# A two-block transformer kernel on one core: weight parts at a pitch of 1028 words, x_high's tiles at 514

## The chip, the cores and the metric

The kernel runs on one core of a Trainium2 chip. The metric is the device time of one execution in microseconds; the time before is 3353.7 us, the median of 3 runs from 3351.68 to 3357.03. Engines go by the names of the profile: PE is TensorE (its weight loads, LDWEIGHTS, are listed apart as PEld), ACT is ScalarE, DVE is VectorE, POOL is GpSimd, SP is SyncE, which issues the DMAs.

## What is computed

Two blocks follow each other, with two layers each, on one sequence of 512 rows with 1024 columns. Cut to what matters here, a layer of the first block is

```python
h = x @ w_in[l]                      # 1024 -> 10016 columns
# four branches of 512 columns: a recurrence, latent attention, a convolution, attention into 256 memory rows
proj = jnp.einsum('bsnc,ncd->bsnd', branches, w_o_branch[l])
merged = jnp.sum(gates * proj, axis=2)      # gates: sigmoid of 4096 columns of h
x = _layer_norm(DEEPNORM_ALPHA * x + merged @ w_out[l], ln_g[l], ln_b[l])
```

and a layer of the second block (which also carries a context of 256 rows, in its first layer through everything, in its second as keys and values only)

```python
zx = hx @ w_in[i]                    # hx: x normed and modulated
mx = concat([latent_attention(...), pool_mix(...), fourier_mix(...)])
x = x + ga1 * (mx @ w_out[i])
x = x + ga2 * swiglu(fx, w_gate_up[i], w_down[i])   # 1024 -> 2 x 2816 -> 1024
```

All of it is float32. The large products are done in three matmuls each: both operands are split into a high part, which the PE takes in its fp32r form, and a low part, the rest; and high x high, high x low and low x high are added up in PSUM.

## The kernel before, in words

**Weights.** All weights of the large products come as chunks of 128 x 1024 words (512 KB), one DMA each, into `ring`, which has three slots. For a chunk that is split, ACT copies the slot to a slot of `highs` (line 123) and POOL subtracts and writes a slot of `lows` (line 131). `highs` and `lows` have two slots each (`PARTS = 2`); split chunks take them in turn, so that every other chunk of a product lies in slot 1. 376 chunks are split.

**Products.** Activations lie transposed, with the 1024 columns of x on 8 tiles of 128 partitions x 512 words: `x_high[:, k, :]` and `x_low[:, k, :]`, k from 0 to 7. For one chunk, the usual order on the PE is 16 matmuls that take `highs` as the stationary operand, with x_high and x_low as the moving one in turn (lines 155 and 158, in `with_high`), and then 8 that take `lows` against x_high (line 723 in the first block, 2140 in the second). The stationary tile of step k is 128 words wide and lies k * 512 bytes into the slot (`tile_of`). Where operands come late, and for `w_out` and `w_down`, all three matmuls of a step k stand together (lines 163, 166 and 167, in `three`). The same two orders run over other activations: `branches_high/low` and `merged_high/low` in the first block (512 columns wide), `context_high/low` (256 wide), `mixed_parts` and `hidden_parts` (512 wide for x, 256 for the context) in the second.

**What sets the order.** Every engine's instructions are written out by hand with semaphores. `Stream.send` issues the DMA of a chunk when its slot of `ring` is free, `Stream.hi` makes the high part on ACT once the chunk of two places earlier has been used, and `Stream.lo` follows on POOL. The PE waits for a high part at the start of a chunk (`wait_high`) and for the low part after the first 16 matmuls (`wait_split`).

**The other matmuls** (the recurrence, both attentions, transposes, small products) take plain float32 operands, such as `ring` itself as the moving operand in line 1544.

**Where tensors lie.** Every tensor has a start address in each partition, and they are laid down one behind another. All moving and stationary operands of the split products start at a multiple of 64 bytes before the change: tiles have a pitch of 2048 bytes (1024 for the context), slots of 4096, and stationary tiles of 512.

Of the kernel before, what the change touches and what calls it, by code (L numbers as in the profile page):

```python
# [17 lines left out]
F32R = mybir.dt.float32r  # L18
# [4 lines left out]
P = 128  # L23
T = 512
D = 1024
DK = D // P
# [14 lines left out]
RING = 3  # L41
PARTS = 2
CW = 1024
# [131 lines left out]
def build(nc, A):  # L175
    with ExitStack() as ctx:
        def sb(name, shape, dt=F32):
            return ctx.enter_context(nc.sbuf_tensor(name, shape, dt))

        pools = [[nc.alloc_semaphore(f"stage{p}_{i}") for i in range(47)] for p in range(3)]  # L180
        arrived = [nc.alloc_semaphore(f"chunk_arrived{i}") for i in range(RING)]
        used = nc.alloc_semaphore("chunks_used")
        hi_made, lo_made = nc.alloc_semaphore("high_made"), nc.alloc_semaphore("low_made")
        loaded = nc.alloc_semaphore("loaded")
        stored = nc.alloc_semaphore("stored")
        constants = nc.alloc_semaphore("second_constants")
        PS = ctx.enter_context(nc.psum_tensor("ps", [P, 8, 512], F32))
        turn = [0]

        def stage():  # L190

            turn[0] += 1
            return Names(pools[turn[0] % 3]), pools[(turn[0] + 1) % 3]

        WR = (sb("ring", [P, RING, CW]), sb("highs", [P, PARTS, CW], F32R), sb("lows", [P, PARTS, CW], F32R),
              arrived, used, hi_made, lo_made)
        mods = sb("mods", [P, LAYERS, 96])

        XH, XL = sb("x_high", [P, DK, T], F32R)[:, :, :], sb("x_low", [P, DK, T], F32R)[:, :, :]
        BR = sb("BR", [P, NB * WT, T])  # L200

        def weights(n):
            if n < SECOND:
                return A["w1"][n // NCHUNK1, n % NCHUNK1, :, :]
            return A["w2"][n - SECOND, :, :]

        split = [NCHUNK1 * layer + n for layer in range(LAYERS) for n in SPLIT1] + SPLIT2
        stream = Stream(WR, weights, split)
        with ExitStack() as one:
            merged = first(nc, one, A, PS, XH, XL, BR, stream, mods, stage, loaded)  # L210
        with ExitStack() as two:
            second(nc, two, A, PS, XH, XL, BR, stream, mods, stage, constants, stored, merged)
# [2888 lines left out]
```

## Time and profile before

| what | value |
|---|---|
| median of 3 runs | 3353.7 us (3351.68 to 3357.03) |
| the profiled execution's own time | 3352.91 us |
| its span, first to last instruction | 3351.1 us |
| mean granted clock of the PE | 0.989 of full speed |
| PE busy | 3206.5 us, 96% |
| PE weight loads busy | 2516.6 us, 75% |
| DVE, ACT, POOL busy | 1508.9, 1183.9, 1485.4 us |

Busy time of the PE counts each matmul to its end, and a matmul of 512 columns is recorded with about 390 ns although the next one starts some 230 ns after it. So what one matmul costs in a dense stretch is read from start to start, over many of them, and not from its duration. A row of the timeline that holds several of one kind gives the start of the first and the time to the end of the last.

### The profile page before, as it was taken

How to read it: one execution, taken by the hardware profiler on the slowest of the kernel's cores; microseconds unless marked ns; L12 is line 12 of the kernel's file. 1: busy time of each engine (PE TensorE's matmuls, PEld its weight loads, DVE VectorE, ACT ScalarE, POOL GpSimd, SP SyncE). 2: the span in 40 equal slices, each digit the busy share in tenths (PEclk: the TensorE clock that was granted, in tenths of full speed). 3: DMA queues.
4: the chain of work that ended last, by engine and by line, in shares of the span. 5: the costliest groups of instructions: out<-in, count | busy, mean ns of one | idle time of the engine just before them, and what ended most of it. 6: DMA issues, size and time to landing. Idle time of an engine off the chain costs nothing. (4 is left out here: it accounts for less than half of the span.)

```text
span 3351.1 us, 51795 instructions
## 1 busy us (share of the span) xinstructions
PE 3206.5 (96%) x21120; PEld 2516.6 (75%) x21120; DVE 1508.9 (45%) x2374; ACT 1183.9 (35%) x1940; POOL 1485.4 (44%) x820
## 2 busy tenths in 40 slices
PE   8899999999999999999998989999999998999999
PEld 6784786888668747868876756788888875678787
DVE  7633374999575333949996235300100022520000
ACT  6224433422353434252225445322122243532221
POOL 4421553444353235545442276344234434745454
PEclk9999999999999999999999999999999999999999
DMA  3011132555220111235543200121122211023232
GB/s 130 8 34 57 57 101 76 208 201 191 78 63 4 46 63 64 94 114 196 206 151 109 66 26 27 51 64 63 57 70 63 63 61 51 16 80 101 92 97 94
DMA packets 77611, 284.18 MB, mean 85 GB/s; under 512 B 8736, under 2 KB 8736, under 8 KB 76864
## 3 DMA queue, kind: packets, MB, share of 16 engines
q1 hardware_dynamic: 77376, 280.88, 25.2%
q8 instruction: 168, 2.75, 0.3%
q14 instruction: 67, 0.55, 0.1%
HBM read 278.75 MB, written 2.10 MB: 84 GB/s over the span
## 5 line engine op out<-in xcount | busy, mean ns | idle before, releaser
L131 POOL TENSOR_TENSOR lows<-ring,highs 128x1024 fp32r<-128x1024 f32 x376 | 941.4, 2505 | 1542.5 <-ACT highs L123 1508.3
L155 PE MATMUL ps<-x_high,highs 128*128 128x512 f32 x2080 | 831.5, 400 | 33.7 <-ACT highs L123 14.9
L158 PE MATMUL ps<-x_low,highs 128*128 128x512 f32 x2080 | 814.3, 391 | 0.0
L123 ACT ACTIVATE highs<-ring 128x1024 fp32r<-128x1024 f32 x376 | 397.0, 1056 | 714.6 <-PE ps L155 375.8
L155 PEld LDWEIGHTS ps<-x_high,highs 128*128 128x128 f32 x2080 | 392.4, 189 | 133.6 <-issue 37.8
L158 PEld LDWEIGHTS ps<-x_low,highs 128*128 128x128 f32 x2080 | 392.8, 189 | 83.8 <-issue 4.8
L1790 DVE CUSTOM_DVE_ANT_0 BR<-BR 128x1024 f32<-128x1024 f32 x144 | 289.4, 2010 | 6.8
L2830 DVE TENSOR_TENSOR hidden_scratch<-ps,hidden_scratch 128x512 f32<-128x512 f32 x44 | 30.4, 691 | 546.5 <-PE ps L2140 538.3
L723 PE MATMUL ps<-x_high,lows 128*128 128x512 f32 x1024 | 252.9, 389 | 0.0
L723 PEld LDWEIGHTS ps<-x_high,lows 128*128 128x128 f32 x1024 | 192.2, 188 | 39.9
L2706 DVE SCALAR_TENSOR_TENSOR BR<-ps,mod,BR 128x512 f32<-128x512 f32 x72 | 47.3, 662 | 364.9 <-PE ps L167 364.9
L163 PE MATMUL ps<-hidden_parts,highs 128*128 128x512 f32 (+1 forms) x528 | 188.0, 356 | 0.0
L167 PE MATMUL ps<-hidden_parts,lows 128*128 128x512 f32 (+1 forms) x528 | 188.0, 356 | 0.0
L166 PE MATMUL ps<-hidden_parts,highs 128*128 128x512 f32 (+1 forms) x528 | 188.0, 356 | 0.0
L471 POOL TENSOR_SCALAR tiles<-tiles 128x768 f32<-128x768 f32 (+1 forms) x80 | 154.8, 1947 | 29.0 <-DVE tiles L498 29.0
L2140 PE MATMUL ps<-x_high,lows 128*128 128x512 f32 x672 | 167.1, 391 | 0.0
L1605 DVE SCALAR_TENSOR_TENSOR ps<-X,par,ps 128x512 f32<-128x512 f32 x232 | 152.9, 741 | 0.0
L2140 PEld LDWEIGHTS ps<-x_high,lows 128*128 128x128 f32 x672 | 123.3, 188 | 24.0
L471 POOL TENSOR_SCALAR X<-X 128x256 f32<-128x256 f32 (+3 forms) x96 | 97.7, 1030 | 67.3 <-DVE X L498 67.2
L492 DVE TENSOR_REDUCE tiles<-ps 128x1 f32<-128x768 f32 (+1 forms) x80 | 67.6, 845 | 109.2 <-PE ps L365 109.0
L166 PEld LDWEIGHTS ps<-hidden_parts,highs 128*128 128x128 f32 x528 | 99.4, 188 | 15.8
L163 PEld LDWEIGHTS ps<-hidden_parts,highs 128*128 128x128 f32 x528 | 99.2, 188 | 16.0
(443 smaller groups left out, 5584.6 us busy)
## 6 DMA issues: line engine op xcount, KB each, us to landing
ring<-in_w SPq DMA_DIRECT2D x414, 512.0 KB, 3.5
BR<-in_ada SPq DMA_DIRECT2D x72, 512.0 KB, 3.5
merging<-in_ada SPq DMA_DIRECT2D x24, 512.0 KB, 3.4
X<-in_xT SPq DMA_DIRECT2D x4, 512.0 KB, 6.5
X<-in_memT SPq DMA_DIRECT2D x2, 1024.0 KB, 5.3
BR<-in_cond SPq DMA_DIRECT2D x4, 512.0 KB, 4.7
out<-BR SPq DMA_DIRECT2D x8, 256.0 KB, 4.5
cst<-in_cst SPq DMA_DIRECT2D x1, 1408.0 KB, 8.0
```

The source lines that it names most:

```text
L123: nc.scalar.activation(self.high(n), self.chunk(n), ACT.Copy).then_inc(self.hi_made, 1)
L131: nc.gpsimd.tensor_tensor(self.low(n), self.chunk(n), self.high(n).bitcast(F32), ALU.subtract).then_inc(self.lo_made, 1)
L155: mm = nc.tensor.matmul(ps, high, xhigh, start=start, stop=False)
L158: nc.tensor.matmul(ps, high, xlow, start=False, stop=False)
L163: mm = nc.tensor.matmul(ps, high, xhigh, start=start, stop=False)
L166: nc.tensor.matmul(ps, high, xlow, start=False, stop=False)
L167: return nc.tensor.matmul(ps, low, xhigh, start=False, stop=stop)
L471: nc.gpsimd.tensor_scalar(prob(i, u), prob(i, u), stats[:, 3, n:n + 1], None, ALU.mult).then_inc(S("normed"), 1)
L723: mm = nc.tensor.matmul(PS[:, bank, :], tile_of(stream.low(n), k), xh[:, k, :], start=False, stop=(k == DK - 1))
L1605: ins = v.scalar_tensor_tensor(out=ACC[:, c, :] if tap == TAPS - 1 else acc, in0=H0[:, c, tap:tap + T], scalar=w, in1=acc, op0=ALU.mult, o ...
L1790: v.tensor_tensor_reduce(PROD, rows_of(t), CB[:, c, :], 1.0, 0.0, ALU.mult, ALU.add, AD[:, t, c:c + 1]).then_inc(S("ada"), 1)
L2140: mm = nc.tensor.matmul(ps, tile_of(stream.low(n), k), high[:, k, :], start=False, stop=(k == DK - 1))
```

## The change

The slots of `highs` and `lows` get a pitch of 1028 words in place of 1024, and the tiles of `x_high` one of 514 words in place of 512. The words that are added are never read or written: the views that the rest of the kernel uses are cut to the old widths.

```diff
-        WR = (sb("ring", [P, RING, CW]), sb("highs", [P, PARTS, CW], F32R), sb("lows", [P, PARTS, CW], F32R),
-              arrived, used, hi_made, lo_made)
+        ring, highs = sb("ring", [P, RING, CW]), sb("highs", [P, PARTS, CW + 4], F32R)
+        lows = sb("lows", [P, PARTS, CW + 4], F32R)
+        WR = (ring, highs[:, :, 0:CW], lows[:, :, 0:CW], arrived, used, hi_made, lo_made)
         mods = sb("mods", [P, LAYERS, 96])
 
-        XH, XL = sb("x_high", [P, DK, T], F32R)[:, :, :], sb("x_low", [P, DK, T], F32R)[:, :, :]
+        XH, XL = sb("x_high", [P, DK, T + 2], F32R)[:, :, 0:T], sb("x_low", [P, DK, T], F32R)[:, :, :]
```

No instruction is added, removed or moved: each engine has the same list in the same order (PE 9604 rows of the program, DVE 1808, ACT 1258, POOL 431, SP 322), each line number behind the change being higher by one. What changes are addresses. The start addresses, in bytes of a partition, with the remainder by 256 in brackets:

| tensor | before | after |
|---|---|---|
| highs, slot 0 / slot 1 | 28800 (128) / 32896 (128) | 28800 (128) / 32912 (144) |
| lows, slot 0 / slot 1 | 36992 (128) / 41088 (128) | 37024 (160) / 41136 (176) |
| x_high, tile k | 45952 + 2048k (128) | 46016 + 2056k (192 + 8k) |
| x_low | 62336 (128) | 62464 (0) |
| branches_high / branches_low | 158464 (0) / 125696 (0) | 158592 (128) / 125824 (128) |
| merged_high / merged_low | 212928 (192) / 196544 (192) | the same |
| context_high / context_low | 127744 (0) / 135936 (0) | 127872 (128) / 136064 (128) |
| mixed_parts, hidden_parts | 163648 (64), 147264 (64) | 163776 (192), 147392 (192) |

So the padding also moves what lies behind it: x_low and most later tensors lie 128 bytes further on. By 64 bytes, slot 1 of `highs` has the remainder 16, the slots of `lows` 32 and 48, and x_high's tile k has 8k; every other operand of the split products still has 0. Among the plain float32 matmuls, line 784 takes as its stationary operand a part of `par` that starts 56 bytes behind a multiple of 64, before as after.

## Rows read from the trace of the kernel before

**Rows 1.** The page: its head and first part, busy time of each engine.
```profile
span 3351.1 us, 51795 instructions
...
PE 3206.5 (96%) x21120; PEld 2516.6 (75%) x21120; DVE 1508.9 (45%) x2374; ACT 1183.9 (35%) x1940; POOL 1485.4 (44%) x820
```

**Rows 2.** The last chain, in order of time: start us, us, what.
```profile
3170.22 1.81 PE ps L2140 x8
3175.66 1.81 PE ps L2140 x8
3181.10 1.81 PE ps L2140 x8
```

**Rows 3.** PE timeline, start us, duration, line: x, then branches, then x.
```profile
1490.92 0.39 PE L155 MATMUL ps<-x_high,highs 128*128 128x512 f32 x1
...
1494.54 1.98 PE L723 MATMUL ps<-x_high,lows 128*128 128x512 f32 x8
1496.36 0.40 PE L155 MATMUL ps<-branches_high,highs 128*128 128x512 f32 x1
...
1501.95 0.39 PE L155 MATMUL ps<-x_high,highs 128*128 128x512 f32 x1
```

**Rows 4.** PE timeline: hidden_parts, 512 wide, and earlier 256 wide.
```profile
3158.04 0.40 PE L163 MATMUL ps<-hidden_parts,highs 128*128 128x512 f32 x1
...
3164.81 0.39 PE L167 MATMUL ps<-hidden_parts,lows 128*128 128x512 f32 x1
...
2663.10 0.28 PE L163 MATMUL ps<-hidden_parts,highs 128*128 128x256 f32 x1
...
2664.12 0.39 PE L163 MATMUL ps<-hidden_parts,highs 128*128 128x512 f32 x1
```

**Rows 5.** PE timeline: merged (two rows), then context, 256 wide.
```profile
888.20 0.39 PE L155 MATMUL ps<-merged_high,highs 128*128 128x512 f32 x1
...
891.86 1.99 PE L1844 MATMUL ps<-merged_high,lows 128*128 128x512 f32 x8
...
2214.31 1.12 PE L2140 MATMUL ps<-context_high,lows 128*128 128x256 f32 x8
2215.26 0.40 PE L155 MATMUL ps<-x_high,highs 128*128 128x512 f32 x1
```

**Rows 6.** Windows: us, busy of PE, PEld, DVE, ACT, POOL, granted clock, DMA.
```profile
1490.92:1496.36 5.44, 5.44 (x26) 4.51 (x25) 5.02 (x7) 5.40 (x9) 2.16 (x1) 1.00 0.65 220
...
3158.04:3164.81 6.77, 6.77 (x31) 5.46 (x29) 0.25 (x1) 1.06 (x1) 2.40 (x1) 1.00 0.00 0
1496.36:1501.95 5.59, 5.59 (x26) 4.51 (x24) 5.59 (x7) 4.05 (x7) 2.29 (x2) 1.00 0.79 288
```

**Rows 7.** PE timeline: a run of plain float32 matmuls (ring moving).
```profile
548.52 5.74 PE L1544 MATMUL ps<-ring,X 128*128 128x512 f32 x13
```

**Rows 8.** Two lines of plain float32 matmuls: durations ns, min/median/max.
```profile
L1544 PE MATMUL ps<-ring,X x64: 592/592/593, 542.9 to 1454.0; 128*128 128x512 f32 x64
...
L784 PE MATMUL ps<-X,par x16: 589/589/694, 27.5 to 932.4; 64*128 64x512 f32 x16
```

**Rows 9.** Groups on the PE, shapes apart: busy us, mean ns, idle before.
```profile
L155 PE MATMUL ps<-x_high,highs 128*128 128x512 f32 x2080 | 831.5, 400 | 33.7 <-ACT highs L123 14.9 <-ACT X L268 7.6 <-DVE x_low L611 5.1
L158 PE MATMUL ps<-x_low,highs 128*128 128x512 f32 x2080 | 814.3, 391 | 0.0
L723 PE MATMUL ps<-x_high,lows 128*128 128x512 f32 x1024 | 252.9, 389 | 0.0
L2140 PE MATMUL ps<-x_high,lows 128*128 128x512 f32 x672 | 167.1, 391 | 0.0
...
L167 PE MATMUL ps<-hidden_parts,lows 128*128 128x512 f32 x352 | 139.2, 396 | 0.0
...
L158 PE MATMUL ps<-context_low,highs 128*128 128x256 f32 x416 | 101.9, 283 | 0.0
...
L1717 PE MATMUL ps<-branches_high,lows 128*128 128x512 f32 x256 | 65.0, 395 | 0.0
L163 PE MATMUL ps<-mixed_parts,highs 128*128 128x512 f32 x128 | 52.1, 407 | 4.6 <-DVE mixed_parts L2702 4.6
```

**Rows 10.** Timelines of PE, ACT and POOL beside the chain's chunks.
```profile
3171.87 0.39 PE L155 MATMUL ps<-x_high,highs 128*128 128x512 f32 x1
...
3172.57 1.05 ACT L123 ACTIVATE highs<-ring 128x1024 fp32r<-128x1024 f32 x1
...
3173.70 2.39 POOL L131 TENSOR_TENSOR lows<-ring,highs 128x1024 fp32r<-128x1024 f32 x1 [3.01 <-ACT highs L123]
```

## The prediction, made before the changed kernel had run

> **What bounds the kernel now.** The page first [rows 1]: the PE is busy 96% of 3351.1 us, and no other engine half of it. So the end is set by how fast the PE gets through its matmuls wherever it doesn't wait. The last chain shows such a place [rows 2]: the 8 matmuls with `lows` come back at 3170.22, 3175.66 and 3181.10, every 5.44 us, and the chain runs from PE to PE. A chunk is 24 matmuls, so one costs 5.44/24 = 226.7 ns. The timeline of another stretch has the same [rows 3]: from 1490.92 to 1496.36, 24 matmuls over x.
>
> The reader should then see that this price isn't the same for all operands. In the next chunk of that timeline, with the same instructions over the branches, 24 matmuls take 1501.95 - 1496.36 = 5.59 us, 232.9 ns each. Over hidden_parts, 29 matmuls from 3158.04 to 3164.81 take 233.4 ns each [rows 4]. The granted clock is 1.00 in all three stretches [rows 6], which is the level of 2.4 GHz, and over hidden_parts the DMA share is 0.00, so neither clock nor transfers make the difference. At 2.4 GHz 512 columns last 213.3 ns: an fp32r matmul pays 13 to 20 ns on top. A plain float32 matmul doesn't: 13 rows of line 1544 take 5.74 us, less the 0.592 that the last one lasts [rows 7, 8], is 429 ns for each of 12, which is two passes of 214.5 ns.
>
> Two things differ between those stretches: tensor and address. By the table of addresses, moving minus stationary operand, taken by 256 bytes, is 0 for x (226.7 ns), 64 for merged, 128 for branches (232.9) and 192 for hidden_parts (233.4). Merged has 16 matmuls from 888.20 to 891.86, 228.8 ns [rows 5]. For 256 columns, 192 (hidden_parts) has 9 from 2663.10 to 2664.12, 113.3 ns [rows 4], and 128 (context) has 8 from 2214.31 to 2215.26, 118.8 ns [rows 5]. I read this as two streams in the SBUF, the moving operand and the stationary tile of the next matmul that is loaded meanwhile, which hold each other up by an amount that hangs on how their addresses lie to each other. It isn't proven: four distances, each with its own tensor.
>
> **The change, part by part.** No instruction goes, comes or moves. Three things can change the time.
>
> *First, new distances for the PE.* I price each by a straight line between the four measured ones (0: 226.7, 64: 228.8, 128: 232.9, 192: 233.4, 256 again 226.7). Counts are those of [rows 9] or follow from the code's order (lines 155, 158 and a third one have 416, 416 and 416 for the context; 163, 166 and 167 the same count each).
> - x_high against `highs` (2080 matmuls, [rows 9]): 64 + 8k in slot 0 and 48 + 8k in slot 1, on average 84: 230.1 ns, +3.4 each, +7.1 us.
> - x_low against `highs` (2080): it isn't padded, but moves by 128 bytes, to 128 and 112: 232.4 ns, +5.7 each, +11.9 us.
> - x_high against `lows` (1024 + 672 + 384 of other lines, 2080): 32 + 8k and 16 + 8k, on average 52: 228.4 ns, +1.7 each, +3.5 us.
> - branches (512 with `highs`, 256 with `lows`): from 128 to 0 and 240 with `highs`, 227.5 ns, and to 224 and 208 with `lows`, 230.9: -2.8 and -0.5 us.
> - hidden_parts and mixed_parts, 512 wide (3 x 352 and 3 x 128): from 192 to 64, 48, 32 and 16: 228.2 ns, -5.2 each, -7.5 us.
> - merged stays at 64 or comes to 48 to 16: -0.3 us.
> - 256 wide: context (1248) goes from 128 to about 0, hidden and mixed (720) from 192 to about 64. No row shows either distance at this width. The two that are shown lie 5.5 ns apart; I take half of that, down for context and up for the others: -3.4 and +2.0 us.
> Together +10.0 us. I count every matmul as lying in a dense stretch. The PE's idle time before line 155 is only 33.7 us over 2080 matmuls [rows 9], so this overstates little.
>
> *Second, starts off a 64-byte boundary.* 7 of 8 x_high tiles and three of four slots of weight parts now start there. A stream of 2048 bytes then touches 33 blocks of 64 bytes and not 32. Bounds: below, nothing, since line 784, whose stationary operand starts 56 bytes behind such a boundary, lasts 589 ns against 592 [rows 8]. Above, one block's worth of columns, 16 at 2.4 GHz or 6.7 ns, for 7/8 of the 4160 matmuls that move x_high: 24 us. That size is no accident of mine alone: 226.7 ns is 544 columns' time, 32 more than the matmul has, and 233.4 is 560, 48 more, so the chip seems to pay in steps of 16. I take a quarter, 6 us: the nearest row shows nothing, but its two slow passes are also those that pay nothing at any address.
>
> *Third, those who write and read the padded tensors.* ACT makes a high part in 1.05 us and POOL a low part in 2.39 [rows 10]. The chunk that starts at 3171.87 is followed by the next one at 3171.87 + 5.44 = 3177.31. The high part is done at 3173.62: 3.7 us to spare. The low part is done at 3176.09 and wanted 16 matmuls into that chunk, at 3180.94: 4.9 us. (The two rows are the parts made while that chunk runs.) Were POOL to take half as long again, 1.2 us more, it would still be hidden. I cost this at nothing; with the cover gone, 1 us for each of 376 chunks would show.
>
> **Sum.** 10.0 + 6 = +16 us. The profiled execution took 3352.9 us, span 3351.1; the median is 3353.7, 0.8 higher. I forecast 3370 us, 0.5% slower, with 3357 to 3395 as this case's own range: 10 alone or less if the lines between the distances are wrong by half, and all 24 of the second term and more above.
>
> **What the Trainium skill says against this.** The Trainium skill, "SBUF — State Buffer", Who interferes with whom, gives the PE two read ports, one for the moving operand and one for weight loads, independent, and says that PE and ACT never wait on anyone. The Trainium skill, "TensorE: Matmul & The Clock Gate", Back-to-back issue gap, gives N/2.4 + 2.5 ns, 215.8 for 512 columns. By these addresses would not matter, and the sum would be 0. The trace agrees for plain float32, 214.5 ns a pass, and not for fp32r, 226.7 to 233.4.
>
> **The rivals.**
> *Faster: the streams no longer meet.* If what costs 13 to 20 ns is that both streams ask for the same place by 64 bytes in the same moment, then different remainders end it. For it: all split operands have remainder 0 now, and all pay. Against it: a matmul moves 2048 bytes of each partition while 512 bytes of weights are loaded, so the two streams pass each other at every offset anyway, and distances that differ by whole multiples of 64 already change the price. One step less on all 6240 matmuls over x, 6.7 ns, is -42 us; with the gains above for branches, hidden and mixed, -11, it gives about 3301. The whole price gone, 11.9 ns for 6240, 18 for 2208 and some 10 for 2350 others, is -138 us, 3216. It decides as soon as x_low and x_high fall below 226.7 ns. Chance 0.31.
> *No change* (where the two pages' rules lead as well). The mechanism would be that the distances are not the cause and the tensors' place in the program is; then x stays at 226.7. Or losses on x and gains on the others cancel: -11 for branches, hidden and mixed against +22 for x lies within the error of my lines. 3347 to 3360. Chance 0.19.
> *Much slower: every start off the boundary costs a full step.* Then 24 us for x_high, and the weight slots make the stationary stream longer too, up to one step more for three quarters of 11,070 matmuls, 55 us. With the 10 of the distances about 3400 to 3440. Chance 0.10.
> The forecast has 0.40.
>
> **How the numbers follow.** About 0.2%, 7 us, can be told from no change. Of the forecast's 0.40, 0.36 is slower and 0.04 the same; of the second rival's 0.19, 0.15 is the same and 0.02 each faster and slower. With the others: slower 0.36 + 0.02 + 0.10 = 0.48, same 0.19, faster 0.31 + 0.02 = 0.33. The range reaches down to the one-step gain, 3305, which leaves out a third of the first rival, and up to 3405, which leaves out most of the third: 0.1 below, 0.08 above.
>
> **What the profile after would show.** The x chunk's period in the last chain tells most: above 5.44 us the forecast holds, at 5.44 the second rival, below it the first. Step by step: x_low's matmuls dearer than x_high's before; the branches chunk down from 5.59 towards 5.5 us; hidden_parts down from 233.4 towards 228 ns; the price of x_high's tiles with k (if the second term is real, k = 0 is cheaper than the rest); line 131 at 2.4 us and line 123 at 1.05. The prediction is wrong if the distance by 256 bytes isn't what sets the price, or if the price follows the remainder by 64.

## The result, and the profile after

The changed kernel takes 3373.26 us (median of 3 runs, 3371.72 to 3379.16), against 3353.7 before: a ratio of 1.0061, 95% interval 1.0038 to 1.0084. It is slower, by some 20 us, and 3 us slower than forecast.

The page's head and part 1 of the kernel after, which answer to [rows 1]. The same number of instructions run. The PE is busy 24 us longer (3230.3 against 3206.5), the DVE 12 us less, the others within 4 us of before.

```profile
span 3371.4 us, 51795 instructions
PE 3230.3 (96%) x21120; PEld 2520.1 (75%) x21120; DVE 1496.9 (44%) x2374; ACT 1184.1 (35%) x1940; POOL 1487.4 (44%) x820
```

The chain that ended last, kernel after, answering to [rows 2] (start us, us, what; line 2141 is line 2140 of before). Two chunks lie between the first row and the second, 11.14 us, and the short rows between are steps of the same chain. A chunk takes 5.57 us, 232.1 ns per matmul, where it took 5.44 and 226.7.

```profile
3193.79 1.88 PE ps L2141 x8
...
3204.93 1.88 PE ps L2141 x8
...
3216.08 1.88 PE ps L2141 x8
...
3227.23 1.88 PE ps L2141 x8
```

Windows of the kernel after (columns as in [rows 6]): a chunk over x, one over the branches, and two of the last chain. The granted clock is 1.00, the level of 2.4 GHz, in all of them, as it was before. In the last one the vector engines and transfers do little (DMA share 0.29), and a chunk over x is as dear as where they are busy (0.69). So neither of them made it dearer.

```profile
1503.24:1508.80 5.56, 5.56 (x25) 4.52 (x24) 5.14 (x7) 5.52 (x9) 2.38 (x1) 1.00 0.69 206
1508.80:1514.40 5.60, 5.60 (x25) 4.54 (x24) 5.45 (x9) 3.92 (x7) 2.01 (x2) 1.00 0.84 296
3193.79:3204.93 11.14, 11.14 (x49) 9.02 (x49) 0.69 (x1) 3.13 (x4) 4.79 (x3) 1.00 0.29 95
```

PE timeline of the kernel after, over hidden_parts, to be held against [rows 4]. From 3164.74 to 3182.78 stand 78 matmuls, 231.3 ns each. It was 233.4 and was to become 228.2.

```profile
3164.74 0.39 PE L167 MATMUL ps<-hidden_parts,lows 128*128 128x512 f32 x1
...
3182.78 0.39 PE L167 MATMUL ps<-hidden_parts,lows 128*128 128x512 f32 x1
```

The costliest groups of the kernel after, answering to [rows 9, 10]. The PE's rows of x grew in mean duration by 2 to 7 ns. ACT's and POOL's writers of weight parts stand at 1057 and 2510 ns for all 376 chunks, where the page of before has 1056 and 2505 ns; their work stays beside the PE's.

```profile
L131 POOL TENSOR_TENSOR lows<-ring,highs 128x1024 fp32r<-128x1024 f32 x376 | 943.4, 2510 | 1559.5 <-ACT highs L123 1523.6
L155 PE MATMUL ps<-x_high,highs 128*128 128x512 f32 x2080 | 836.4, 402 | 29.1 <-ACT highs L123 10.5
L158 PE MATMUL ps<-x_low,highs 128*128 128x512 f32 x2080 | 824.1, 396 | 0.0
L123 ACT ACTIVATE highs<-ring 128x1024 fp32r<-128x1024 f32 x376 | 397.1, 1057 | 734.2 <-PE ps L155 396.4
...
L724 PE MATMUL ps<-x_high,lows 128*128 128x512 f32 x1024 | 260.5, 396 | 0.0
...
L2141 PE MATMUL ps<-x_high,lows 128*128 128x512 f32 x672 | 170.8, 396 | 0.0
```

**Where the 20 us are.** The PE runs its 21,120 matmuls in the same order in both traces, so the time from each start to the next can be compared one by one. Of the span's +20.3 us, +28.6 lie in dense stretches over x: x_high with `lows` +13.0, x_low with `highs` +10.3, x_high with `highs` +5.3. In five places of before, 1.0 to 1.7 us pass from the start of the last matmul of the branches with `lows` to the next one over x, with the PE idle; after the change 0.23 us does, and that gave 5.2 back. All else together is -3.

**The price by class.** The table has the mean time from start to start in ns, over all matmuls of a class in dense stretches (its own gap and the eight before it under 250 ns), worked out from each trace; the numbers of the experiments are told below. Under it stands the distance (moving minus stationary start, by 256 bytes). A gap is put down to the matmul that starts it. Where two classes alternate, as x_high and x_low do with `highs`, that is a convention: their mean is sure, which of the two is the dear one isn't.

| class | before | after | shift_only | behind128 | behind64 | behind32 | weights_only | x_tiles_only |
|---|---|---|---|---|---|---|---|---|
| x_high, highs | 227.7 | 230.4 | 234.3 | 233.9 | 229.2 | 233.6 | 231.0 | 231.8 |
| distance | 0 | 48 to 120 | 64 | 128 | 64 | 32 | 64, 48 | 0 to 56 |
| x_low, highs | 227.3 | 232.6 | 230.0 | 231.3 | 229.0 | 233.1 | 230.7 | 231.7 |
| distance | 0 | 128, 112 | 128 | 128 | 64 | 32 | 64, 48 | 0 |
| x_high, lows | 227.5 | 233.9 | 231.0 | 232.8 | 229.4 | 233.2 | 230.8 | 230.3 |
| distance | 0 | 16 to 88 | 64 | 128 | 64 | 32 | 32, 16 | 0 to 56 |
| hidden, highs, 512 wide | 233.1 | 231.9 | 228.8 | 228.1 | 228.1 | 233.3 | 234.4 | 228.0 |
| distance | 192 | 64, 48 | 64 | 64 | 0 | 224 | 0, 240 | 0 |

### The profile page after: what moved, and what is told of

Same layout as the page of the kernel before. It is cut to its first block and busy times, and to the rows that moved or that the text cites. A ratio compares the mean times of both kernels' runs of the same rounds, so it can differ in the third digit from the quotient of the medians.

```text
span 3371.4 us, 51795 instructions
## 1 busy us (share of the span) xinstructions
PE 3230.3 (96%) x21120; PEld 2520.1 (75%) x21120; DVE 1496.9 (44%) x2374; ACT 1184.1 (35%) x1940; POOL 1487.4 (44%) x820
## 5 line engine op out<-in xcount | busy, mean ns | idle before, releaser
L131 POOL TENSOR_TENSOR lows<-ring,highs 128x1024 fp32r<-128x1024 f32 x376 | 943.4, 2510 | 1559.5 <-ACT highs L123 1523.6
L155 PE MATMUL ps<-x_high,highs 128*128 128x512 f32 x2080 | 836.4, 402 | 29.1 <-ACT highs L123 10.5
L158 PE MATMUL ps<-x_low,highs 128*128 128x512 f32 x2080 | 824.1, 396 | 0.0
L123 ACT ACTIVATE highs<-ring 128x1024 fp32r<-128x1024 f32 x376 | 397.1, 1057 | 734.2 <-PE ps L155 396.4
L1791 DVE CUSTOM_DVE_ANT_0 BR<-BR 128x1024 f32<-128x1024 f32 x144 | 278.7, 1935 | 6.8
L724 PE MATMUL ps<-x_high,lows 128*128 128x512 f32 x1024 | 260.5, 396 | 0.0
L2141 PE MATMUL ps<-x_high,lows 128*128 128x512 f32 x672 | 170.8, 396 | 0.0
L167 PEld LDWEIGHTS ps<-hidden_parts,lows 128*128 128x128 f32 x528 | 99.1, 188 | 15.8
L163 PEld LDWEIGHTS ps<-hidden_parts,highs 128*128 128x128 f32 x528 | 99.2, 188 | 15.6
```

The source lines that it names most:

```text
L123: nc.scalar.activation(self.high(n), self.chunk(n), ACT.Copy).then_inc(self.hi_made, 1)
L131: nc.gpsimd.tensor_tensor(self.low(n), self.chunk(n), self.high(n).bitcast(F32), ALU.subtract).then_inc(self.lo_made, 1)
L155: mm = nc.tensor.matmul(ps, high, xhigh, start=start, stop=False)
L158: nc.tensor.matmul(ps, high, xlow, start=False, stop=False)
L163: mm = nc.tensor.matmul(ps, high, xhigh, start=start, stop=False)
L167: return nc.tensor.matmul(ps, low, xhigh, start=False, stop=stop)
```

## The experiments

### Whole multiples of 64 bytes only

Four kernels. The first shifts tensors as the change does but keeps every start on a 64-byte boundary. The second puts all tensors behind `lows` 128 bytes further. The third puts the weights and all behind them 128 bytes further, so that no distance changes except those to merged_high and merged_low, which lie at fixed places. The fourth takes from the change only the pitch of the weights' slots.

```diff
 shift_only
+        sb("pad", [P, 16])
         mods = sb("mods", [P, LAYERS, 96])
...
+        sb("pad2", [P, 16])          # between x_high and x_low
 behind128
+        sb("pad", [P, 32])
         mods = sb("mods", [P, LAYERS, 96])
 before_ring128
+        sb("pad", [P, 32])
         WR = (sb("ring", [P, RING, CW]), sb("highs", [P, PARTS, CW], F32R), sb("lows", [P, PARTS, CW], F32R),
 weights_only
+        ring, highs = sb("ring", [P, RING, CW]), sb("highs", [P, PARTS, CW + 4], F32R)
+        lows = sb("lows", [P, PARTS, CW + 4], F32R)
+        WR = (ring, highs[:, :, 0:CW], lows[:, :, 0:CW], arrived, used, hi_made, lo_made)
```

> No pitch changes; 64 bytes of padding behind lows and 64 behind x_high, so that every tensor starts at the same remainder by 256 as in the change (x_high 192, x_low 0, branches and context 128, hidden_parts 192) while all operands stay on 64-byte boundaries. Theory A (the distance of moving and stationary operand by 256 bytes sets the price): x_high 228.8 ns a matmul, x_low 232.9, branches 226.7, hidden_parts 228.8; about +10 us, 3364. Theory C (only the remainder by 64 matters): nothing changes, 226.7 for x, 3354. Rival B (the price belongs to the tensor's place in the program, not its address): 3354 as well, and branches stay at 232.9.

> 128 bytes of padding between lows and all that follows, all on 64-byte boundaries: both x tensors at distance 128, branches and context at 0, hidden_parts at 64, merged unchanged at 64. Theory A: x 232.9 ns (+39 us over 6240 matmuls), branches 226.7 (-5 us), hidden_parts and mixed_parts 228.8 (-7 us): about 3381. Theories B and C: 3354, x at 226.7.

> 128 bytes of padding ahead of ring: the weight slots and everything behind them move together, so the distances of x, branches, context and hidden_parts stay and only merged's (which is laid down from the other end) goes from 64 to 192. If the distance sets the price (A): x at 226.7 ns, merged at 233.4, 3355 in all. If it is the moving operand's own address by 256: the same as the kernel with 128 bytes behind lows, x at 232.9 and 3381.

> Only highs and lows get the pitch of 1028 words. Distances: x against highs 64 and 48, against lows 32 and 16; branches and context 192 and 176 against highs, hidden_parts 0 and 240. Theory A alone: x 228.5 with highs and 227.5 with lows (+9 us), hidden and mixed -7, context -6 or so: about 3350. If a weight slot's start off a 64-byte boundary costs by itself, the matmuls with lows stand at 232 ns or above instead of 227.5 and those of highs' slot 1 above those of slot 0: 3365 or more.

Measured: shift_only 3364.87 us, ratio 1.0035 (1.0022 to 1.0048). behind128 3368.06, 1.0040 (1.0026 to 1.0053). before_ring128 3353.45, 1.0004 (0.9994 to 1.0013). weights_only 3364.92, 1.0039 (1.0024 to 1.0054).

Only before_ring128 came out as expected in every part. shift_only met its 3364, but by luck: x_high with `highs`, at distance 64, cost 234.3 ns and not 228.8, x_low at 128 cost 230.0 and not 232.9. behind128 missed its 3381 by 13 us: its x matmuls, all at 128, cost 231.3 to 233.9, so that the dense stretches over x grew by 30 us where 39 were expected, and 4 us of waits behind the branches went. weights_only came out at the 3365 of the theory that a start off a boundary costs, but not by its price: with `lows` x cost 230.8 where that theory had 232 or more and the distance by straight lines 227.5.

The last chain of behind128, one chunk a row: 5.57 or 5.58 us, as after the change, with no start off a 64-byte boundary.

```profile
3233.83 1.86 PE ps L2141 x8
3239.41 1.86 PE ps L2141 x8
3244.98 1.86 PE ps L2141 x8
3250.56 1.87 PE ps L2141 x8
```

PE timeline of before_ring128 over merged_high and merged_low, to be held against [rows 5]. The distance went from 64 to 192. From 873.08 to 876.81 stand 16 matmuls, 233.1 ns each, where it was 228.8.

```profile
873.08 0.40 PE L155 MATMUL ps<-merged_high,highs 128*128 128x512 f32 x1
...
876.81 0.40 PE L1845 MATMUL ps<-merged_high,lows 128*128 128x512 f32 x1
```

What follows: in before_ring128 nearly everything moved and x, branches and hidden kept their prices (227.4, 237.1, 233.1); only the class whose distance changed changed its price. So the place and the tensor's part in the program don't set the price; how moving and stationary operand lie to each other does. It isn't the matmul's own distance alone, though: x_high at 64 costs 234.3 in shift_only and 229.2 in behind64, where x_low is at 64 too, and hidden_parts with `highs`, at 0 and 240 in weights_only, stays at 234.4. A tensor that comes from distance 192 to 64 gets cheaper (hidden 233.1 to 228.1 in behind128), and x, which is the one at distance 0, can only lose.

### The tiles of x_high alone, and 64 bytes more

x_tiles_only lays x_low first, where it keeps distance 0, and x_high behind it with its pitch of 514 words. behind64 is behind128 with 16 words.

```diff
 x_tiles_only
-        XH, XL = sb("x_high", [P, DK, T], F32R)[:, :, :], sb("x_low", [P, DK, T], F32R)[:, :, :]
+        XL = sb("x_low", [P, DK, T], F32R)[:, :, :]
+        XH = sb("x_high", [P, DK, T + 2], F32R)[:, :, 0:T]
 behind64
+        sb("pad", [P, 16])
         mods = sb("mods", [P, LAYERS, 96])
```

> Only x_high's tiles get the pitch of 514 words; x_low is laid down ahead of x_high, so that it stays at distance 0 on a 64-byte boundary, and x_high's tile k has distance 8k from the weight slots. Branches and context come to distance 192, hidden_parts and mixed_parts to 0. If only the distance by 256 counts: x_low 227 ns, x_high 227.6, hidden_parts 227: about 3349. If a start off a 64-byte boundary costs by itself: the matmuls of x_high with lows at 231 ns or above, as the 233.9 of the change, and those with highs above 228: 3360 or more.

> 64 bytes of padding behind lows, all on 64-byte boundaries: both x tensors at distance 64, branches and context at 192, hidden_parts and mixed_parts at 0. Distance theory, prices from the aligned stretches so far: x 229 to 231 ns (+13 to +22 us), hidden_parts and mixed_parts down from 233 to about 227 (-9), branches unchanged at 233: 3357 to 3366. If hidden_parts stays at 233 at distance 0, the price is not the distance's alone.

Measured: x_tiles_only 3357.47 us, ratio 1.0013 (1.0004 to 1.0023). behind64 3355.53, 1.0002 (0.9993 to 1.0011). behind64 came 1.5 us under its range of 3357 to 3366, with x at 229.0 to 229.4 and hidden_parts at 228.1, as the distances had it. The total of x_tiles_only lies between what the theories expected, since both signs are in it: +22.7 us in dense stretches over x, and -5.8 over hidden_parts, -6.6 over the context and -5.2 of waits. Two things in its prices were new. x_high's tiles at distance 0 (k = 0) are no cheaper with `highs` than the rest, 232.4 ns against 227.0 to 238.0; with `lows` k = 0 is the cheapest, 224.4 against 227.6 to 236.6. And x_low, at distance 0 for every k, costs 231.7 in place of 227.3: the matmuls beside it in the order have a part in its price. Whichever of the two the gaps are put down to, their mean rose to 231.8.

### Moving the branches and hidden_parts to distance 0

If distances set the price, x should stay where it is and the dear tensors be moved. rooms128 puts 128 bytes behind x_low (branches at distance 0, hidden at 64), rooms64 64 bytes (branches at 192, hidden at 0).

```diff
 rooms128 (rooms64: 16 in place of 32)
+        sb("pad", [P, 32])
         BR = sb("BR", [P, NB * WT, T])
```

> 128 bytes of padding behind x_low only: x stays at distance 0 (227 ns), branches and context come to 0, hidden_parts and mixed_parts to 64. Distance theory: branches from 233 to about 228 (-4 us), hidden_parts and mixed_parts from 233 to 229 (-6 us): about 3343, faster than both kernels. If the price belongs to the tensor's place in the program: 3353.

> 64 bytes of padding behind x_low only: x at distance 0, hidden_parts and mixed_parts at 0, branches and context at 192. Distance theory: hidden_parts and mixed_parts 227 ns (-9 us), branches 233 as before, context's 256-wide matmuls 118 to 120 ns: about 3344.

Measured: rooms128 3354.2 us, ratio 1.0002 (0.9993 to 1.0012), a miss by 11 us. rooms64 3347.88, 0.9983 (0.9974 to 0.9993). The prices came as expected: in rooms128 the branches' classes went from 237.3, 228.4 and 233.4 to 226.6, 226.7 and 226.7, in rooms64 hidden_parts from 233.1 to 228.0 with `highs` and from 233.2 to 226.7 with `lows`. The time of rooms128 didn't follow, and rooms64 was 4 us above its 3344.

Windows over the stretch in which the branches' outputs are gated and merged, in the two layers of the first block, before and rooms128 (columns as in [rows 6]). First the kernel before, then rooms128.

```profile
602.00:855.00 253.00, 251.58 (x1097) 205.31 (x1096) 240.23 (x259) 73.92 (x87) 120.97 (x45) 1.00 0.54 189
1505.00:1765.00 260.00, 256.05 (x1111) 207.77 (x1110) 245.54 (x261) 71.88 (x84) 126.84 (x46) 1.00 0.54 186
```

```profile
601.00:854.00 253.00, 246.45 (x1084) 202.80 (x1082) 242.88 (x258) 72.88 (x85) 126.27 (x45) 1.00 0.54 189
1505.00:1762.00 257.00, 248.36 (x1091) 204.12 (x1090) 245.57 (x259) 73.67 (x86) 125.51 (x45) 1.00 0.53 186
```

Before, the PE stood idle for 5.4 us in the two windows (513 less 507.6), in rooms128 for 15.2 (510 less 494.8); the DVE is busy 95 and 96%. What the PE, the transfers and ACT wait for in rooms128 from 600 to 855 us (engine, line, released by; us, times, longest):

```profile
PE ps L155 <- ACT highs L123: 4.7, 3, 1.6
```

```profile
SPq L1690 <- DVE mods L1791: 162.2, 43, 6.8
SPq L112 <- POOL lows L131: 36.4, 12, 5.7
```

```profile
ACT highs L123 <- DMA ring<-in_w: 14.3, 6, 4.4
```

SP holds its queue 162 us for line 1791 of the DVE (156 in before, 114 in after), which has to free a slot before the next transfer of another operand. The weights of the PE are issued behind that on the same queue, and ACT, which splits them, waits for their arrival 14.3 us (5.7 before in that stretch). So in rooms128 the chain of waits leads from the PE back to the DVE. Matmul by matmul, its dense stretches over branches, hidden_parts and mixed_parts 512 wide gave 10.5 us back against before, and the waits behind the branches with `lows` took 7.1 and those over merged 4.0.

In after it is the other way round: over the two layers the PE is idle 0.6 us of 511 and the DVE busy 92%, so the PE sets the pace there. From the first to the last matmul of branches with `lows` the two layers take 245.3 and 247.5 us before, 246.5 and 246.6 after, 246.5 and 248.5 in rooms128, and 248.4 in both in behind32 (below), where all cost 233 to 235 ns and the PE is idle 0.6 us too. Before stands close to the point where the two engines meet: dearer matmuls first use up its 5.4 us of idle time, and cheaper ones are paid back in waits. That the DVE is what holds the stretch in rooms128 is read from these waits; no run made the DVE faster.

### The price measured by itself

price runs only matmuls, 48 per setting, alternating between two source lines; no other engine works meanwhile. Weights tiles lie 512 bytes apart from a start on a multiple of 256 bytes, moving tiles 2048 apart from a start a number of bytes further, and some settings differ from that as the table says.

```python
for r in range(48):
    k = r % 8
    mov = X[:, x0 + k * pitch:x0 + k * pitch + n]
    wt = W[:, w0 + k * 128:w0 + (k + 1) * 128]
    mm = one(nc, PS[:, i % 8, 0:n], wt, mov, r == 0, r == 47)
```

> A kernel that measures the price of a matmul alone: it computes none of the reference (its output is zeros) and runs 2,000-odd matmuls in groups of 48, each group with one setting of weights' and moving side's places, and nothing else running beside them. Distances are of the moving side's start minus the weights' start, by 256 bytes. Theory one (the distance sets the price, a settled pattern in whole steps of 16 columns): at distances 0, 64, 128 and 192 about 227, 229, 233 and 233 ns, 256 columns about 113, 114, 119 and 114 ns, plain float32 the same at both distances; when weights and moving side are moved together off a 64-byte boundary, the price stays that of distance 0. Theory two (a start off a 64-byte boundary costs in itself, about one step of 16 columns, 6.7 ns): distances 16, 32 and 48 dearer than both 0 and 64, and both moved together dearer still. Theory three (nothing but other engines' traffic to the memory makes the price): all settings at 213 to 216 ns.

The PE timeline of price: distances 16, 32, 48, 64, 80, 96 in this order. From one start to the next, divided by 48: 231.7, 233.3, 233.3, 229.2, 230.8 ns.

```profile
26.66 11.28 PE L20 MATMUL ps<-x,weights 128*128 128x512 f32 x48
37.78 11.37 PE L16 MATMUL ps<-x,weights 128*128 128x512 f32 x48
48.98 11.36 PE L20 MATMUL ps<-x,weights 128*128 128x512 f32 x48
60.18 11.16 PE L16 MATMUL ps<-x,weights 128*128 128x512 f32 x48
71.18 11.25 PE L20 MATMUL ps<-x,weights 128*128 128x512 f32 x48
82.26 11.38 PE L16 MATMUL ps<-x,weights 128*128 128x512 f32 x48
```

The settings, as means of start to start over the last 32 matmuls of each, ns:

| distance, bytes | 0 | 16 | 32 | 48 | 64 | 80 | 96 | 112 |
|---|---|---|---|---|---|---|---|---|
| 512 columns | 226.7 | 231.6 | 233.3 | 233.4 | 228.9 | 231.0 | 233.3 | 231.3 |
| distance, bytes | 128 | 144 | 160 | 176 | 192 | 208 | 224 | 240 |
| 512 columns | 232.3 | 233.4 | 234.3 | 233.3 | 233.4 | 234.6 | 233.4 | 226.7 |

| other settings | ns |
|---|---|
| distances 8, 24, 40, 56 | 233.3, 232.5, 234.2, 232.8 |
| distance 0, both moved by 16, 32, 128 bytes | 231.1, 226.7, 226.7 |
| weights alone moved by 16 bytes (distance 240) | 233.3 |
| pitch 514 words, from distance 0, 64, 128, 192 | 230.8, 234.5, 232.2, 232.5 |
| 256 columns, distance 0, 64, 128, 192 | 120.0, 117.8, 118.7, 113.3 |
| plain float32, half of a row's 429.2, distance 0 and 128 | 214.6, 214.6 |
| two moving tensors in turn, each with the same weights tile: distances 0 and 0, 64 and 64, 128 and 128, 192 and 192 | 226.7, 228.8, 232.3, 233.3 |
| the same, distances 64 and 128 | 233.5 |
| the same, the first with a pitch of 514 words: distances 0 and 0, 64 and 128 | 232.3, 232.3 |

The rows with two moving tensors show the part of the neighbours with nothing else at work. Alone, distances 64 and 128 cost 228.9 and 232.3, 230.6 in the mean; in turn they cost 233.5, in gaps of 237.3 behind the one at 64 and 229.4 behind the one at 128. That is the pattern of shift_only (234.3 and 230.0). And a tensor at distance 0 with a pitch of 512, whose own price is 226.7, makes 232.3 in turn with one at a pitch of 514, whose own is 230.8. From 376.34 to 382.41 stand 26 matmuls, 233.5 ns each:

```profile
376.34 0.40 PE L16 MATMUL ps<-x,weights 128*128 128x512 f32 x1
376.58 0.39 PE L16 MATMUL ps<-y,weights 128*128 128x512 f32 x1
...
382.41 0.40 PE L16 MATMUL ps<-x,weights 128*128 128x512 f32 x1
```

The 48 plain float32 matmuls of a setting leave 96 rows of 429.2 ns, so that one costs 858 ns, not the 429 of one row.

The third theory, that other engines' traffic makes the price, is out: with none, the prices are those of the kernels. The second is out as it was put, since both moved by 32 bytes stay at 226.7. The first holds for the four distances that it had, and not where it said that only the distance counts: with both moved by 16 bytes the price is 231.1. The straight line between 0 and 64 that the prediction drew is wrong, since 16 to 48 are dearer than both its ends.

### A constant 32 bytes, and the best layout

```diff
 behind32
+        sb("pad", [P, 8])
         mods = sb("mods", [P, LAYERS, 96])
 rooms64_hidden (rooms64, and the context's tiles of hidden_parts 64 bytes later)
-        hidden = room.enter_context(nc.sbuf_tensor(f"hidden_parts{layer}", [P, 33 * T], F32R))
+        hidden = room.enter_context(nc.sbuf_tensor(f"hidden_parts{layer}", [P, 33 * T + 16], F32R))
...
-               "c": (tiles_of(hidden, 22, 2 * FH, CTX)[:, 0:FH, :], tiles_of(hidden, 22, 2 * FH, CTX)[:, FH:2 * FH, :])}
+               "c": (tiles_of(hidden[:, 16:], 22, 2 * FH, CTX)[:, 0:FH, :], tiles_of(hidden[:, 16:], 22, 2 * FH, CTX)[:, FH:2 * FH, :])}
```

> Before with 8 words (32 bytes) in front of all tensors behind the weights' low parts: every moving tile lies at a constant distance off a 64-byte boundary (x 32, hidden_parts 224, branches and context 160), weights stay on boundaries. If only varying remainders break the settled pattern, x costs between what 0 and 64 cost (227 to 229.5 ns), the hidden_parts between 227 and 233, the total is 3345 to 3358. If a start off a boundary costs in itself, as in the changed kernel (x_high with highs 230.4, x_low with highs 232.6, x_high with lows 233.9 ns), the 1194 dense x matmuls cost 3 to 6 ns more each and the others as much: 3360 to 3372.

> As rooms64 (16 words behind x_low, hidden_parts at distance 0, branches at 192), and the 256-wide tiles of hidden_parts that meet the context's weights begin 16 words later, at distance 64. By the distances, their 528 matmuls fall from 119.3 to 113.7 ns each, 3.0 us: 3345. If the pace there is set by the supply of weights, the 3 us go into waits and the time is that of rooms64, 3348.

Measured: behind32 3384.11 us, ratio 1.0084 (1.0071 to 1.0098), the slowest of all. A constant remainder is no better than a varying one. Its x matmuls cost 233.1 to 233.6 ns, what price has for distance 32. My idea that only varying remainders hurt fell with this run. Its last chain, a chunk a row, 5.60 us each:

```profile
3230.83 1.87 PE ps L2141 x8
3236.43 1.87 PE ps L2141 x8
3242.03 1.87 PE ps L2141 x8
```

rooms64_hidden 3346.81 us, ratio 0.9971 (0.9959 to 0.9984), beside 0.9983 (0.9974 to 0.9993) of rooms64. Both are faster than either kernel of this study. What the extra 64 bytes bring isn't settled: the intervals overlap, most of the distance between the ratios lies in the runs of before that they are held against (median 3355.71 and 3352.96), and the 256-wide tiles of hidden_parts fell only from 119.3 to 117.7 ns with `highs` and from 120.0 to 118.6 with `lows`, 0.8 us in all, not to 113.7.

### The chunks over x played alone

replay runs the chunks over x at the addresses of eight of the kernels, 8 chunks for each layout, with nothing else on the core, and then groups of 256 columns behind groups of 512.

```python
for k in range(8):
    with_high(nc, ps, at(hi + s + 512 * k, P), at(xh + pitch * k, T), k == 0)
    with_xlow(nc, ps, at(hi + s + 512 * k, P), at(xl + 2048 * k, T))
for k in range(8):
    with_low(nc, ps, at(lo + s + 512 * k, P), at(xh + pitch * k, T), k == 7)
```

> A kernel that plays the matmuls alone: it computes none of the reference (its output is zeros), no engine but the PE works and no transfer runs. For each of eight layouts (before, after, shift_only, weights_only, x_tiles_only, behind128, behind64, behind32) it runs 8 chunks over x, each 8 pairs of a tile of highs with x_high and x_low and then 8 tiles of lows with x_high, at the very addresses that these tensors have in that kernel. If the addresses of the two streams set the price by themselves, the chunk's period is that of the kernels: before 227.5 ns per matmul, 5.46 us a chunk; after 232.3, 5.58; shift_only 231.8, 5.56; weights_only 230.8, 5.54; x_tiles_only 231.3, 5.55; behind128 232.7, 5.58; behind64 229.2, 5.50; behind32 233.3, 5.60. If the writers of highs and lows, the vector engines or transfers had a part in it, the layouts lie closer together or all at 5.44. Behind them it runs matmuls of 256 columns in groups of 24, each behind 16 of 512 columns, at distances 64, 0, 192 and 128, each behind the four distances of the wide ones: by distance alone 117.8, 120.0, 113.3 and 118.8 ns (those of the first three as measured alone, the last as over context); if the pattern that the PE is in when it arrives matters too, as the 256-wide tiles of hidden_parts (113.7 or 117.7 at one address) suggest, one distance gives two prices.

The chain of replay; its rows with x8 are the 8 matmuls with `lows`, one chunk from each to the next. The first three are before's layout (5.44 us a chunk), the next three after's (5.57 and 5.58), the last three behind32's (5.60).

```profile
44.15 1.81 PE ps L36 x8
49.59 1.81 PE ps L36 x8
55.03 1.81 PE ps L36 x8
...
88.28 1.88 PE ps L36 x8
93.85 1.87 PE ps L36 x8
...
99.43 1.88 PE ps L36 x8
...
354.89 1.87 PE ps L36 x8
...
360.49 1.87 PE ps L36 x8
...
366.09 1.87 PE ps L36 x8
```

| layout | replay: mean | x_high, highs | x_low, highs | x_high, lows | the kernel's mean |
|---|---|---|---|---|---|
| before | 226.7 | 226.8 | 226.6 | 226.6 | 227.5 |
| after | 232.1 | 229.8 | 232.7 | 233.9 | 232.3 |
| shift_only | 231.7 | 235.2 | 229.5 | 230.2 | 231.8 |
| weights_only | 230.9 | 231.5 | 230.6 | 230.4 | 230.8 |
| x_tiles_only | 231.1 | 231.6 | 231.6 | 230.1 | 231.3 |
| behind128 | 233.3 | 237.2 | 229.4 | 233.4 | 232.7 |
| behind64 | 228.9 | 229.3 | 228.9 | 228.5 | 229.2 |
| behind32 | 233.3 | 232.1 | 234.5 | 233.4 | 233.3 |

The addresses alone give the kernels' mean prices within 0.8 ns, and most classes within 1. In behind128 and behind32 single classes lie up to 3.3 ns apart, in ways that cancel in the mean. By replay the change costs 6240 x 5.46 ns = 34.1 us over x; 28.6 were found in the dense stretches of the trace.

At 256 columns one distance has two prices. These are rows of the same chain: groups of 24 matmuls of 256 columns at distance 192 (line 44), behind 16 of 512 columns at distance 64 and then at 128 (line 40). The first group takes 2.83 us, 117.9 ns each, the second 2.73, 113.8.

```profile
432.47 3.68 PE ps L40 x16
436.15 2.83 PE ps L44 x24
438.98 3.72 PE ps L40 x16
442.70 2.73 PE ps L44 x24
```

## Why the prediction was right, and where not

**What bounds the kernel** held. No instruction came or went, and what the matmuls over x took more is what the time grew by, less what waits gave back.

**That the distance sets the price** was put as unproven, and is shown for the addresses of the streams together: by before_ring128, where the place changed and only merged's distance did, and by price and replay, where nothing but matmuls ran. It fails as the prediction put it, one price for each distance: in shift_only and in price, distances 64 and 128 in turn cost more than the mean of the two alone. By the Trainium skill, "SBUF — State Buffer", Who interferes with whom, the PE has two independent read ports and never waits on anyone. If that means that addresses don't matter, the runs disagree for fp32r operands, 226.7 to 234.6 ns with nothing else at work, and agree for plain float32, 429.2 ns a row at both distances tried. No run shows which port or memory the time is spent in.

**First term, x.** Forecast with `highs` 230.1 for x_high and 232.4 for x_low; measured 230.4 and 232.6. That they fit so well is partly luck: at 80, 96 and 112 the line has 229.8, 230.9 and 231.9, price 231.0, 233.3 and 231.3, and in shift_only x_high at 64 and x_low at 128 cost 234.3 and 230.0. With `lows` it was 228.4 against 233.9, and that step failed: the straight line between 0 and 64. Price has 231.6 to 233.4 at 16, 32 and 48. It cost 11.4 us of error (2080 x 5.5 ns). The counts leave out 192 matmuls over x in lines 163, 166 and 167, about 1 us.

**First term, the gains.** They were to be 12.5 us, and by measured price and count they are 0.6. Hidden_parts 512 wide came to 231.9 with `highs` and 230.8 with `lows`, mixed_parts to 232.3 and 230.9, in place of 228.2 (-2.1 us together, not -7.5), by the same straight line, since two thirds of these matmuls are at distances of 48, 32 and 16. The branches brought 1.4 us, not 3.3: with `lows` their tiles at 224 and 208 cost 233.0 and 233.4, not 230.9, and at 240 with weights that are off by 16 bytes 233.1 to 233.3, as price has it. The context brought 0.2 and not 3.4; half of the gap between two measured rows was no estimate of a distance that neither showed. Hidden and mixed 256 wide lost 2.6 us, against 2.0 forecast. Merged, at 230.5 to 230.9 in place of 229.0, lost 0.6.

**Second term, 6 us for starts off a boundary.** Its mechanism, one block of 64 bytes more, isn't what the chip does: both streams moved by 32 bytes cost nothing. But something finer than 64 bytes does count. Distances of 16 to 48 cost 4.9 to 6.7 ns more than 0 in price, as much as the prediction's upper bound of one step, and a weights tile off by 16 bytes costs 4.4 at distance 0. The whole rise over x by measured prices is 2080 x (2.7 + 5.3 + 6.4) = 30 us, beside 22.5 and 6 forecast. So the sum over x was nearly right with its parts put in the wrong places.

**Third term**, the writers hidden, held: 1057 and 2510 ns, and the last chain runs from PE to PE.

**What the sum left out** is the stretch where the PE isn't the bound. The prediction counted every matmul as dense because the idle time before line 155 was small [rows 9]. In the merging stretch of before the PE is idle 5.4 us and the DVE busy 95%, with SP's queue waiting for it, so that the PE could take 5.2 us longer over its matmuls there before the time grew. The same DVE kept nearly all of the gain from rooms128. The missing gains and these waits have opposite signs; the total came out within 3 us partly by that.

**The rivals.** That the streams no longer meet, falls: no x class fell below 227 ns in after, and no distance in price lies below 226.7. No change falls too, with replay's 5.44 and 5.57 us. That every off-boundary start costs a full step comes near for a constant distance of 32 (behind32, +30 us), and not for the change, which has distances of 64 to 128 among its own. That k = 0 would be cheaper with x_high was wrong: in after, with `highs` it is the dearest, 231.8 against 228.7 to 231.3, and with `lows` it has 230.5 at k = 0 and 230.0 at k = 7, with up to 239.2 between.

**Open.** Why these distances and not others; price only maps them. That a matmul's price depends on its neighbours' addresses (x_low in x_tiles_only, 64 and 128 in turn in price) and on what ran before (256 columns) suggests a state that is carried from matmul to matmul, which these runs don't identify. Whether rooms64_hidden is faster than rooms64 is open too.

## What to carry to other kernels

When the PE is the bound and a matmul costs more than its columns, read its price from start to start by class of operands, and hold it against the start addresses of the moving and the stationary tile: here 7 ns in 227 hung on nothing else, and 64 bytes of padding at the right place, which left the best tensor alone and moved the dear ones, made the kernel 0.2 to 0.3% faster, where padding the best one cost 0.6%. Measure such a price alone, at each setting and in the order in which the kernel alternates its operands, before summing with it: a line between four points missed a hump between the first two, and two distances in turn cost more than their mean. And price a gain only over stretches in which the engine sets the pace.

## What the runs showed of the hardware

- With nothing else running, an fp32r matmul of 512 columns costs from 226.7 to 234.6 ns by the distance of its two operands' starts, by 256 bytes; 0 and 240 are the best, most others 231 to 234. Distances 64 and 128 in turn cost 233.5, where each alone costs 228.9 and 232.3. A plain float32 matmul leaves two rows of 429.2 ns, at both distances tried.
- Several settled prices are whole steps of 16 columns at 2.4 GHz: 226.7 ns is 544 columns' time, 228.9 is 549.3 (a third of a step), 233.3 is 560.
- Pads that vary the remainder from tile to tile don't average between good and bad: from distance 0 a pitch of 514 words costs 230.8 where 512 costs 226.7.
- At 256 columns the best distance isn't that of 512: 192 has 113.3 ns, 0 has 120.0. And at 192 the price is 113.4 or 117.7, by which matmuls ran before.
